# Two state-space heads in one block, one-pass broadcasts, and the decay's differences on VectorE

## Chip, cores and metric

The kernel runs on one core of a Trainium2 chip. The metric is device time in microseconds of one execution. All arithmetic is fp32, or fp32 split into a rounded high part and a low part (the type fp32r) for the large projections.

## What is computed

Two blocks of two layers work on 512 positions of width 1024. The change lies in the first layer of the second block, a state-space mixer with 32 heads of dimension 64 in 4 groups of 8, a state of 128, and the 512 positions in 4 chunks of 128:

```python
dt = softplus(dt + dt_bias);  da = dt * -exp(a_log)
xdt = xs * dt
a_cs = cumsum(da, axis=2)                 # inside each chunk of 128
decay = exp(where(l >= s, a_cs[l] - a_cs[s], -inf))
cb = einsum('bclgn,bcsgn->bcgls', cm, bm)
y_diag = einsum('bcgls,bcgrls,bcsgrp->bclgrp', cb, decay, xdt)
states = einsum('bclgn,bclgr,bclgrp->bcgrpn', bm, exp(a_cs[-1] - a_cs), xdt)
# prev: states carried from chunk to chunk
y_off = einsum('bclgn,bcgrpn,bclgr->bclgrp', cm, prev, exp(a_cs))
y = (y_diag + y_off + d_skip * xs) * silu(z)
y = rms_norm(y, by group of 512 channels) * norm_w;  out = y @ w_out
```

## The kernel before

Five engines work from their own queues, with semaphores between them, and the order on each queue is written out by hand. Channels stand in the 128 partitions and positions in the 512 columns. Weights come through a ring of four blocks; GpSimd splits each into `w_hi` and `w_lo` (L411, L413). A projection tile of 128 channels is 8 steps (`tile_steps`, L840), and a step is three matmuls of 128x512 (L476, L479, L482). The projections z (gate), B, C and x of the mixer are computed one group ahead: `steps_of(ahead, n)` lets n steps run between other work, so that TensorE has something to do while the other engines prepare a head. In group 3 only its own 32 z steps are left.

For each group g, TensorE (L932) transposes B, makes `cb` = B^T C chunk by chunk, broadcasts head 0's cumulated decay, transposes x (`xt`, read by VectorE as `xdt` and `wx`), and makes the three state products (`st`, L957). The sum of the previous group's squares (`norm_sum`) lies between the first and the second of these, because the small products take turns in two PSUM banks, ps6 and ps7: `misc` (L856) lets a product wait until the one before the last has been read from the bank. This stretch, up to the first head, is called the lead below. Then come the 8 heads:

- `spread` (L862, L866 and L867): a column of `ident_r`, repeated 128 times, times `cs_hi` and then times `cs_lo` puts the cumulated decay of one head into all partitions of ps3.
- `decays` on ScalarE (L1432): for each of the 4 chunks a Relu of csT - ps3 into `seg` (L1438), then Exp of ps3 into `ctu` (L1440), which frees ps3, and Exp of -seg (L1442).
- `decayed` on VectorE (L2229): `seg` times `cb`, `ctu` times C.
- `head` on TensorE (L869): for each chunk `xdt` times `seg`, and from the second chunk on the carried state `hst` times `ctu`, added on top; 7 matmuls. An fp32 matmul stands as two records in the trace, so a head has 14. Head r writes partitions 0 to 63 of its bank if r is even and 64 to 127 if it is odd: 64 of the 128 columns of the array.
- `pair` on VectorE (L2207): once two heads are there, adds the skip term, multiplies by Silu of z; ScalarE squares (`gated_square`), VectorE adds up (`add_squares`), and in the next group `norm_root` (L1450) and `group_norm` (L2235, with a reciprocal and four scalings) finish the norm.

`seg` and `ctu` have two buffers. On VectorE the conv taps of the next group (`conv_sides`, L2156) stand in between. ScalarE changes its function table between Exp, Silu and Sqrt; Relu, Copy, Identity and Square need no change.

## Time and profile before

| | us |
|---|---|
| median of 3 runs | 2882.8 (2881.3 to 2891.0) |
| the profiled execution | 2888.4 |
| its span | 2886.6 |
| PE (TensorE matmul) busy | 2800.2, 97% |
| DVE (VectorE) busy | 1727.6, 60% |
| ACT (ScalarE) busy | 791.0, 27% |
| POOL (GpSimd) busy | 1732.4, 60% |

The mixer's four groups lie at 1310 to 1601 us of the span. A busy PE says that matmuls are in flight, not how fast they are issued; matmuls overlap, so their cost on the queue is the distance from one start to the next, not the duration shown. In the chain that ended last TensorE has 84% and VectorE 8%. PEclk is TensorE's granted clock as a share of full speed.

### The profile page before, as it was taken

To read this page: it belongs to the slowest core of one execution; us is meant where nothing else is said; L and a number is where in the kernel's file an instruction comes from. 1 tells how busy PE (TensorE), PEld (TensorE's weight loads), DVE (VectorE), ACT (ScalarE), POOL (GpSimd) and SP (SyncE) were. 2 spreads that over 40 slices of the span, in tenths; PEclk is the share of its full clock that TensorE was granted. 3 is DMA by queue.
4 is the path that set the end of the run, shared out by engine and by line. 5 is a ranking of instruction groups with operands and counts; after the bars stand their busy time and mean duration, and the time that the engine had idled before them with its cause. 6 is when DMAs were issued, how large, how long until landed. Compare 5 with 4: busy or idle time off the path is not lost.

```text
span 2886.6 us, 37343 instructions
## 1 busy us (share of the span) xinstructions
PE 2800.2 (97%) x13446; PEld 2271.8 (79%) x13446; DVE 1727.6 (60%) x1974; ACT 791.0 (27%) x1299; POOL 1732.4 (60%) x984
## 2 busy tenths in 40 slices
PE   8899999999899999999998999999999998999999
PEld 6778888888787888877776778888877776788887
DVE  6886766427867665264665558054567776832635
ACT  3434222103443222025555322010222222310202
POOL 5784666666966666754443548666464443666664
PEclk9999999999999999999999999999999999999999
DMA  4201323332012223322111223222231211222321
GB/s 148 66 30 66 95 94 99 105 97 95 23 54 90 97 95 101 103 84 71 61 64 51 69 71 114 98 95 95 73 108 59 67 60 57 84 100 95 98 98 59
DMA packets 66484, 237.45 MB, mean 82 GB/s; under 512 B 7264, under 2 KB 7520, under 8 KB 66336
## 3 DMA queue, kind: packets, MB, share of 16 engines
q1 hardware_dynamic: 65504, 234.00, 24.8%
q8 instruction: 89, 1.46, 0.2%
q10 hardware_dynamic: 832, 1.51, 0.2%
q14 instruction: 59, 0.48, 0.1%
HBM read 233.38 MB, written 2.10 MB: 82 GB/s over the span
## 4 chain that ended last, share of the span: by engine, by line
PE 84%; DVE 8%; DVEq 3%; issue 3%; ACT 1%; POOL 0%; DMA 0%; ACTq 0%; SPq 0%; POOLq 0%
PE ps L476 25%; PE ps L482 24%; PE ps L479 24%; PE ps L1137 1%; DVE qw L2487 1%; PE ps L879 1%; PE ps L639 1%; DVE ps L1786 1%; PE ps L997 1%; PE ps L989 1%; PE ps L992 1%; PE ps L1173 1%; PE ps L882 1%; PE ps L957 0%; DVEq L1905 0%
## 5 line engine op out<-in xcount | busy, mean ns | idle before, releaser
L411 POOL TENSOR_SCALAR w_hi<-w_raw 128x1024 fp32r<-128x1024 f32 x437 | 482.1, 1103 | 1100.0 <-PE ps L476 1013.0
L413 POOL TENSOR_TENSOR w_lo<-w_raw,w_hi 128x1024 fp32r<-128x1024 f32 x437 | 1100.6, 2519 | 36.5
L476 PE MATMUL ps<-x_hi,w_hi 128*128 128x512 f32 x1864 | 746.2, 400 | 26.3 <-DVE x_lo L1658 5.3
L482 PE MATMUL ps<-x_hi,w_lo 128*128 128x512 f32 x1864 | 730.0, 392 | 0.0
L479 PE MATMUL ps<-x_lo,w_hi 128*128 128x512 f32 x1864 | 729.6, 391 | 0.0
L476 PEld LDWEIGHTS ps<-x_hi,w_hi 128*128 128x128 f32 x1864 | 352.4, 189 | 115.0 <-issue 14.0
L482 PEld LDWEIGHTS ps<-x_hi,w_lo 128*128 128x128 f32 x1864 | 352.2, 189 | 75.6
L479 PEld LDWEIGHTS ps<-x_lo,w_hi 128*128 128x128 f32 x1864 | 352.7, 189 | 74.4 <-issue 4.1
L476 PE MATMUL ps<-a_hi,w_hi 128*128 128x512 f32 x512 | 200.0, 391 | 0.0
L482 PE MATMUL ps<-a_hi,w_lo 128*128 128x512 f32 x512 | 199.2, 389 | 0.0
L479 PE MATMUL ps<-a_lo,w_hi 128*128 128x512 f32 x512 | 199.2, 389 | 0.0
L2311 DVE SCALAR_TENSOR_TENSOR xres<-xres,ps 128x512 f32<-128x512 f32 x32 | 22.0, 688 | 241.1 <-PE ps L482 241.1
L2394 DVE TENSOR_TENSOR sqf<-rl 128x512 f32<-128x512 f32 x64 | 110.0, 1719 | 77.4 <-ACT rl L1561 77.4
L2043 DVE SCALAR_TENSOR_TENSOR yz<-ps,prm,yz 128x511 f32<-128x511 f32 x88 | 65.4, 749 | 150.8 <-ACT yz L1359 150.8
L1561 ACT ACTIVATE rl<-ps 128x512 f32<-128x512 f32 x64 | 38.3, 599 | 402.0 <-PE ps L482 369.8
L2397 DVE TENSOR_TENSOR a_lo<-sqf,a_hi 128x512 f32 x64 | 137.5, 2148 | 14.1 <-issue 13.6
L476 PE MATMUL ps<-f_hi,w_hi 128*128 128x512 f32 x352 | 136.9, 389 | 0.0
L479 PE MATMUL ps<-f_lo,w_hi 128*128 128x512 f32 x352 | 136.9, 389 | 0.0
L482 PE MATMUL ps<-f_hi,w_lo 128*128 128x512 f32 x352 | 136.9, 389 | 0.0
L1786 DVE SCALAR_TENSOR_TENSOR ps<-upad,prm,ps 128x512 f32<-128x512 f32 x168 | 117.4, 749 | 7.1 <-issue 6.9
L2080 DVE TENSOR_TENSOR yz<-sgz,yz 128x512 f32<-128x512 f32 x44 | 113.8, 2586 | 0.0
L476 PE MATMUL ps<-xg_hi,w_hi 128*128 128x512 f32 x256 | 111.6, 436 | 1.6 <-DVE xg_lo L2412 1.6
(424 smaller groups left out, 4678.6 us busy)
## 6 DMA issues: line engine op xcount, KB each, us to landing
w_raw<-wts SPq DMA_DIRECT2D x437, 512.0 KB, 3.4
xres<-xT SPq DMA_DIRECT2D x2, 1024.0 KB, 8.3
outT<-xres SPq DMA_DIRECT2D x8, 256.0 KB, 2.1
pf<-pT ACTq DMA_DIRECT2D x2, 512.0 KB, 3.8
prm<-prm SPq DMA_DIRECT2D x1, 452.0 KB, 3.9
lev<-levels ACTq DMA_DIRECT2D x1, 384.0 KB, 3.9
wtmp<-pos SPq DMA_DIRECT2D x1, 128.0 KB, 3.2
ident<-identity SPq DMA_DIRECT2D x1, 64.0 KB, 10.1
```

Source lines behind the costliest of these rows:

```text
L411: nc.gpsimd.tensor_scalar(w_hi[:, s, :], w_raw[:, s, :], 1.0, 0.0, ALU.mult, ALU.add).then_inc(w_rounded[s], 1)
L413: nc.gpsimd.tensor_tensor(w_lo[:, s, :], w_raw[:, s, :], w_hi[:, s, :].bitcast(F32), ALU.subtract).then_inc(w_split[s], 1)
L476: mm = nc.tensor.matmul(out, whi, xhi, start=first, stop=False)
L479: mm = nc.tensor.matmul(out, whi, xlo, start=False, stop=False)
L482: return nc.tensor.matmul(out, wlo, xhi, start=False, stop=last)
L639: mm = nc.tensor.matmul(ps[5][:, qt * VW:(qt + 1) * VW], p_t[:, h % 2, kt, qt * P:(qt + 1) * P], v_sb[:, kt, h, :], start=kt == 0, stop=kt ...
L1561: AC.activation(rl[:, j % 2, :], ps[j][:, :], ACT.Relu).then_inc(relu_ready, 1)
L1786: ins = V.scalar_tensor_tensor(a if k < CONV_K - 1 else yconv[:, c, :], upad[:, c, k:k + S], w, a, ALU.mult, ALU.add)
L2043: V.scalar_tensor_tensor(yv[:, 1:S], ps[b + z][:, 0:S - 1], prm[:, pc + (L_FW + f * 3), :], yv[:, 1:S], ALU.mult, ALU.add).then_inc(side, 1)
L2080: V.tensor_tensor(yz[i % 2][1], sgz[:, :], yz[i % 2][1], ALU.mult).then_inc(f_ready, 1)
L2394: V.tensor_tensor(sqf[:, j % 2, :], rl[:, j % 2, :], rl[:, j % 2, :], ALU.mult).then_inc(acc_free[j], 1)
L2397: V.tensor_tensor(a_lo[:, q * 4 + j, :], sqf[:, j % 2, :], a_hi[:, q * 4 + j, :].bitcast(F32), ALU.subtract).then_inc(a_split, 1)
```

## The change

The two passes of a broadcast become one: `cs_hl` holds the high part in rows 0 to 31 and the low part in rows 32 to 63, and the columns of `ident_r` have ones in both. VectorE makes all of a head's differences in one instruction (`gap`), ScalarE rectifies them in one Relu over 128x512. The matmuls of two heads stand in one block and alternate between the two halves of the array's columns. `seg` and `ctu` get four buffers, so a broadcast goes out up to two heads before its use. `group_norm` is cut into four parts. To make room for the buffers, some small tiles move into tiles that are free at that time.

```diff
-        seg, _ = at("seg", [P, 2, S])
-        ctu, _ = at("ctu", [P, 2, S - P])
-        cs, _ = at("cs", [P, S])
-        cs_hi, _ = at("cs_hi", [P, S], F32R)
-        cs_lo, _ = at("cs_lo", [P, S], F32R)
+        seg, _ = at("seg", [P, 4, S])
+        ctu, _ = at("ctu", [P, 4, S - P])
+        cs_hl, _ = at("cs_hl", [P, S], F32R)
...
             def spread(g, r):
                 k = GH * g + r
                 pe.wait_ge(csb_read, k)
+                pe.wait_ge(gap_ready, k)
                 col = ident_r[:, k:k + 1].to_broadcast([P, P])
-                nc.tensor.matmul(ps[3][:, :], col, cs_hi[:, :], start=True, stop=False)
-                nc.tensor.matmul(ps[3][:, :], col, cs_lo[:, :], start=False, stop=True).then_inc(csb_done, 1)
+                nc.tensor.matmul(ps[3][:, :], col, cs_hl[:, :], start=True, stop=True).then_inc(csb_done, 1)
...
+            def head_pair(g, p):
+                n, out = GT * g + p, ps[4 + p % 2]
+                pe.wait_ge(m_ready, 2 * n + 2)
...
+                both = [(r, slice((r % 2) * HD, (r % 2 + 1) * HD)) for r in (2 * p, 2 * p + 1)]
                 for tt in range(TT):
+                    c = slice(tt * P, (tt + 1) * P)
+                    for r, rows in both:
+                        mm = nc.tensor.matmul(out[rows, c], xdt[:, tt, r * HD:(r + 1) * HD], seg[:, r % 4, c],
+                                              start=True, stop=tt == 0)
                     if tt:
+                        for r, rows in both:
+                            mm = nc.tensor.matmul(out[rows, c], hst[:, tt - 1, r * HD:(r + 1) * HD],
+                                                  ctu[:, r % 4, (tt - 1) * P:tt * P], start=False, stop=True)
                 mm.then_inc(yh_done, 1)
...
+                    if c == 0:
+                        spread(g, 1)
                     if c == 0 and g:
                         norm_sum(g - 1)
...
-                for r in range(GH):
-                    steps_of(ahead, (4 if g else 3) if some else 2)
-                    if r + 1 < GH:
-                        spread(g, r + 1)
-                    steps_of(ahead, (4 if g else 3) if some else 1)
-                    head(g, r)
-            steps_of(ahead, len(TILES) * KD)
+                for p in range(GT):
+                    share = [4 if g else 3] * 4 if some else [2, 1, 2, 1]
+                    steps_of(ahead, share[0])
+                    if p + 1 < GT:
+                        spread(g, 2 * p + 2)
+                    steps_of(ahead, share[1])
+                    if some or p + 1 < GT:
+                        head_pair(g, p)
+                    steps_of(ahead, share[2])
+                    if p + 1 < GT:
+                        spread(g, 2 * p + 3)
+                    steps_of(ahead, share[3])
+            head_pair(GROUPS - 1, GT - 1)
...
             def decays(g, r):
...
-                if k >= 2:
-                    act.wait_ge(yh_done, k - 1)
-                for tt in range(TT):
-                    AC.activation(seg[:, r % 2, tt * P:(tt + 1) * P], ps[3][:, tt * P:(tt + 1) * P], ACT.Relu,
-                                  bias=csT[:, tt, k:k + 1], scale=-1.0)
-                AC.activation(ctu[:, r % 2, :], ps[3][:, P:], ACT.Exp).then_inc(csb_read, 1)
-                act.wait_ge(csb_read, k + 1)
-                AC.activation(seg[:, r % 2, :], seg[:, r % 2, :], ACT.Exp, scale=-1.0).then_inc(dec_ready, 1)
+                if k >= 4:
+                    act.wait_ge(yh_done, k // 2 - 1)
+                AC.activation(ctu[:, r % 4, :], ps[3][:, P:], ACT.Exp).then_inc(csb_read, 1)
+                act.wait_ge(gap_ready, k + 1)
+                AC.activation(seg[:, r % 4, :], seg[:, r % 4, :], ACT.Relu)
+                act.drain()
+                AC.activation(seg[:, r % 4, :], seg[:, r % 4, :], ACT.Exp, scale=-1.0).then_inc(dec_ready, 1)
...
+                decays(g, 1)
                 if g:
                     norm_root(g - 1)
...
-            V.tensor_copy(ident_r[:, :], ident[:, 0:SH])
+            V.tensor_tensor(ident_r[:, :], ident[:, 0:SH], ident[:, SH:2 * SH], ALU.add)
...
-            V.tensor_tensor(cs_lo[:, :], cs[:, :], cs_hi[:, :].bitcast(F32), ALU.subtract).then_inc(small_dve, 1)
+            V.tensor_tensor(cs_hl[SH:2 * SH, :], cs[0:SH, :], cs_hl[0:SH, :].bitcast(F32), ALU.subtract).then_inc(small_dve, 1)
...
+            def gap(g, r):
+                k = GH * g + r
+                dve.wait_ge(csb_read, k + 1)
+                if k >= 4:
+                    dve.wait_ge(yh_done, k // 2 - 1)
+                V.tensor_tensor(seg[:, r % 4, :].rearrange("p (t q) -> p t q", t=TT), csT[:, :, k:k + 1].to_broadcast([P, TT, P]),
+                                ps[3][:, :].rearrange("p (t q) -> p t q", t=TT), ALU.subtract).then_inc(gap_ready, 1)
...
+                gap(g, 0)
                 decayed(g, 0)
+                gap(g, 1)
                 for c in (1, 2):
...
+                decayed(g, 1)
+                gap(g, 2)
                 for r in range(GH):
+                    if r >= 2 and r % 2 == 0:
+                        pair(g, r // 2 - 1)
+                    if 1 <= r < GH - 1:
+                        decayed(g, r + 1)
                     if g + 1 < GROUPS and r >= 3:
                         conv_sides(g + 1, CONV_T[r - 3])
-                    if r >= 2 and r % 2 == 0:
-                        pair(g, r // 2 - 1)
-                    if r + 1 < GH:
-                        decayed(g, r + 1)
                     if r in (5, 7):
                         add_squares(g, (r - 3) // 2)
-                    if r == 1 and g:
-                        group_norm(g - 1)
+                    if 1 <= r < GH - 2:
+                        gap(g, r + 2)
+                    if 1 <= r <= GT and g:
+                        group_norm(g - 1, r - 1)
```

Three places show what moves. TensorE first, the matmuls of heads in group 1, from a projection matmul to the next one (ps4 is the bank of the heads' output; a count says how many alike follow each other). Before, one head:

```order
L482 MATMUL ps0<-x_hi_53,w_lo_51 128x512
L879 MATMUL ps4<-seg_116,xdt_109 64x128 x2
L882 MATMUL ps4<-ctu_117,hst_111 64x128
L879 MATMUL ps4<-seg_116,xdt_109 64x128
L882 MATMUL ps4<-ctu_117,hst_111 64x128
L879 MATMUL ps4<-seg_116,xdt_109 64x128
L882 MATMUL ps4<-ctu_117,hst_111 64x128
L476 MATMUL ps0<-x_hi_53,w_hi_50 128x512
```

After, two heads:

```order
L482 MATMUL ps2<-x_hi_53,w_lo_51 128x512
L881 MATMUL ps4<-seg_116,xdt_109 64x128 x4
L885 MATMUL ps4<-ctu_117,hst_111 64x128 x2
L881 MATMUL ps4<-seg_116,xdt_109 64x128 x2
L885 MATMUL ps4<-ctu_117,hst_111 64x128 x2
L881 MATMUL ps4<-seg_116,xdt_109 64x128 x2
L885 MATMUL ps4<-ctu_117,hst_111 64x128 x2
L476 MATMUL ps2<-x_hi_53,w_hi_50 128x512
```

The same rows now hold two heads: each count is doubled, and within a count the output alternates between partitions 0 to 63 and 64 to 127.

ScalarE in the lead of group 1, from head 0's decay to the root of the previous group's norm, with the semaphores that a row waits for. Before:

```order
L1438 ACTIVATE seg<-ps,csT 128x128 [waits yh_done,csb_done]
L1438 ACTIVATE seg<-ps,csT 128x128 x3
L1440 ACT_TABLE_LOAD
L1440 ACTIVATE ctu<-ps 128x384
L1442 ACTIVATE seg<-seg 128x512 [waits csb_read]
L1496 ACTIVATE hst<-ps 128x512 [waits misc_done]
L1453 ACT_TABLE_LOAD
L1453 ACTIVATE root<-ps,consts 128x512 [waits misc_done]
```

After:

```order
L1448 ACT_TABLE_LOAD [waits yh_done]
L1448 ACTIVATE ctu<-ps 128x384 [waits csb_done]
L1450 ACTIVATE seg<-seg 128x512 [waits gap_ready]
L1452 ACTIVATE seg<-seg 128x512
L1506 ACTIVATE hst<-ps 128x512 [waits misc_done]
L1448 ACTIVATE ctu<-ps 128x384 [waits yh_done,csb_done]
L1450 ACTIVATE seg<-seg 128x512 [waits gap_ready]
L1452 ACTIVATE seg<-seg 128x512
L1463 ACT_TABLE_LOAD
L1463 ACTIVATE root<-ps,consts 128x512 [waits misc_done]
```

Head 1's three rows now stand ahead of the table load and the root, and head 0's Relu waits for VectorE (`gap_ready`).

VectorE in group 1, from the last state addition to the second pair of heads' products. Before:

```order
L2278 TENSOR_TENSOR hst<-hst,ps 128x512 [waits misc_done]
L2232 TENSOR_TENSOR seg<-seg,cb 128x512 [waits dec_ready]
L2233 TENSOR_TENSOR ctu<-ctu,cT 128x384
L2232 TENSOR_TENSOR seg<-seg,cb 128x512 [waits dec_ready]
L2233 TENSOR_TENSOR ctu<-ctu,cT 128x384
L2237 RECIPROCAL rstd<-root 128x512 [waits root2_ready]
L2241 SCALAR_TENSOR_TENSOR y<-y,prm,rstd 128x512 x4
L2211 SCALAR_TENSOR_TENSOR xs<-xs,prm,ps 128x512 [waits sz_ready,yh_done]
L2214 TENSOR_TENSOR y<-xs,y 128x512
L2232 TENSOR_TENSOR seg<-seg,cb 128x512 [waits dec_ready]
L2233 TENSOR_TENSOR ctu<-ctu,cT 128x384
```

After:

```order
L2299 TENSOR_TENSOR hst<-hst,ps 128x512 [waits misc_done]
L2251 TENSOR_TENSOR seg<-seg,cb 128x512 [waits dec_ready]
L2252 TENSOR_TENSOR ctu<-ctu,cT 128x384
L2245 TENSOR_TENSOR seg<-csT,ps 128x512 [waits yh_done,csb_read]
L2251 TENSOR_TENSOR seg<-seg,cb 128x512 [waits dec_ready]
L2252 TENSOR_TENSOR ctu<-ctu,cT 128x384
L2245 TENSOR_TENSOR seg<-csT,ps 128x512 [waits yh_done,csb_read]
L2257 RECIPROCAL rstd<-root 128x512 [waits root2_ready]
L2260 SCALAR_TENSOR_TENSOR y<-y,prm,rstd 128x512
L2222 SCALAR_TENSOR_TENSOR xs<-xs,prm,ps 128x512 [waits sz_ready,yh_done]
L2225 TENSOR_TENSOR y<-xs,y 128x512
L2251 TENSOR_TENSOR seg<-seg,cb 128x512 [waits dec_ready]
```

The subtractions (seg<-csT,ps) are new; the reciprocal and the first scaling stand behind head 3's subtraction and ahead of the first pair's output, and the other three scalings are spread over the following heads.

## Rows read from the trace of the kernel before

**Rows 1.** Windows: length; busy PE, PEld, DVE, ACT, POOL; PEclk; DMA
```profile
1310.13:1378.76 68.63, 68.51 (x355) 54.10 (x353) 39.07 (x51) 38.63 (x76) 27.51 (x16) 1.00 0.21 69
1378.76:1460.16 81.40, 80.56 (x405) 63.57 (x404) 50.79 (x64) 43.99 (x81) 36.20 (x20) 1.00 0.20 64
...
1541.59:1601.48 59.89, 52.34 (x260) 39.00 (x259) 34.21 (x46) 36.71 (x70) 14.17 (x8) 0.91 0.11 38
```

**Rows 2.** PE in time, one head of group 1: start us, us, instruction
```profile
1427.25 0.39 PE L482 MATMUL ps<-x_hi,w_lo 128*128 128x512 f32 x1
1427.57 0.65 PE L879 MATMUL ps<-seg,xdt 128*64 128x128 f32 x4
...
1429.24 0.50 PE L476 MATMUL ps<-x_hi,w_hi 128*128 128x512 f32 x1
1429.58 0.39 PE L479 MATMUL ps<-x_lo,w_hi 128*128 128x512 f32 x1
```

**Rows 3.** PE in time, next broadcast and matmul behind
```profile
1432.11 0.40 PE L866 MATMUL ps<-cs_hi,ident_r 128*128 128x512 f32 x1
...
1432.58 0.39 PE L476 MATMUL ps<-x_hi,w_hi 128*128 128x512 f32 x1
```

**Rows 4.** PE in time, later mixer: alternating halves, then one half
```profile
2199.64 0.69 PE L1137 MATMUL ps<-qw,kw 128*64 128x64 f32 x16
2200.25 0.50 PE L476 MATMUL ps<-xg_hi,w_hi 128*128 128x512 f32 x1
...
2202.65 0.68 PE L1150 MATMUL ps<-qw,kw 128*64 128x64 f32 x8
2203.26 0.50 PE L476 MATMUL ps<-xg_hi,w_hi 128*128 128x512 f32 x1
```

**Rows 5.** Lines: shapes, count; busy us, mean ns; idle before, releaser
```profile
L1438 ACT ACTIVATE seg<-ps,csT 128x128 f32<-128x128 f32 x128 | 36.6, 368 | 68.3 <-PE ps L867 68.0 <-issue 0.2
...
L1442 ACT ACTIVATE seg<-seg 128x512 f32<-128x512 f32 x32 | 20.2, 632 | 1.0
...
L1440 ACT ACTIVATE ctu<-ps 128x384 f32<-128x384 f32 x32 | 16.0, 501 | 0.2
...
L2232 DVE TENSOR_TENSOR seg<-seg,cb 128x512 f32<-128x512 f32 x32 | 25.0, 781 | 77.3 <-ACT seg L1442 76.8
...
L2233 DVE TENSOR_TENSOR ctu<-ctu,cT 128x384 f32<-128x384 f32 x32 | 19.3, 604 | 0.0
```

**Rows 6.** Single lines: count; ns at least/median/at most; first and last start; form
```profile
L2264 DVE TENSOR_TENSOR xdt<-ps,dtT x16: 691/692/693, 1317.9 to 1554.5; 128x512 f32<-128x512 f32 x16
...
L2214 DVE TENSOR_TENSOR y<-xs,y x16: 691/693/2782, 1341.4 to 1603.8; 128x512 f32<-128x512 f32 x16
```

**Rows 7.** ACT in order of time, lead of group 1
```profile
1392.85 0.60 ACT L1496 ACTIVATE hst<-ps 128x512 f32<-128x512 f32 x1 [3.55 <-PE ps L957]
1393.55 1.28 ACT L1453 ACT_TABLE_LOAD   x1
1394.84 0.69 ACT L1453 ACTIVATE root<-ps,consts 128x512 f32<-128x512 f32 x1
```

**Rows 8.** DVE in order of time, lead of group 1
```profile
1391.70 0.69 DVE L2264 TENSOR_TENSOR xdt<-ps,dtT 128x512 f32<-128x512 f32 x1
```

**Rows 9.** PE in time, group 1: first transpose, third state product, head
```profile
1378.76 0.55 PE L937 MATMUL ps<-ident,bT 128*128 128x128 f32 x3
...
1396.46 1.02 PE L957 MATMUL ps<-wx,b_l 128*128 128x512 f32 x2
...
1404.04 0.65 PE L879 MATMUL ps<-seg,xdt 128*64 128x128 f32 x4
```

**Rows 10.** PE in time, group 3: fourth head and matmul behind
```profile
1580.26 1.12 PE L879 MATMUL ps<-seg,xdt 128*64 128x128 f32 x4 [3.92 <-DVE ctu L2233]
...
1583.26 0.50 PE L476 MATMUL ps<-x_hi,w_hi 128*128 128x512 f32 x1
```

**Rows 11.** DVE in order of time, group 3: the reciprocal
```profile
1570.14 3.35 DVE L2237 RECIPROCAL rstd<-root 128x512 f32<-128x512 f32 x1
```

55 lines of the change are left out of this document (25 added, 30 removed).

## The prediction, made before the kernel ran

> **What bounds the kernel now.** I read the stretch table first. The change only touches the state-space mixer, which fills 291 us of the span in four groups [rows 1]. In groups 0 and 1 TensorE is busy for 68.5 of 68.6 and 80.6 of 81.4 us (group 2 repeats group 1), while VectorE is at 39 and 51 us and ScalarE at 39 and 44 us: there TensorE is the bound, and what is taken off its queue shortens the group, as long as nobody makes it wait. Group 3 is another case: 52.3 of 59.9 us at a granted clock of 0.91. It has no next group's projections to fill with, so TensorE already waits there for the decay factors.
>
> Then the price of the parts on TensorE. Every head has a block of 14 matmul records between projection matmuls. The last projection matmul before it starts at 1427.25, the first behind it at 1429.24 and the next at 1429.58 [rows 2]; less two ordinary pitches of 0.23, the block costs 1429.58 - 1427.25 - 0.46 = 1.87 us. Every head also has a broadcast of two passes, 1432.11 to 1432.58, so 0.23 each [rows 3]. A projection step, three matmuls at that pitch, is 0.69 us.
>
> **Part 1: broadcasts of one pass.** The high and the low part stand in rows 0 to 31 and 32 to 63 of one operand, and the selecting column has two ones. It removes 32 passes of 0.23 us: 7.4 us, all on TensorE's queue.
>
> **Part 2: two heads in one block.** A head's output uses half of the array's columns (128*64); the halves of heads 2p and 2p+1 now alternate. Does the chip run them side by side? The trace of before holds both patterns in the later mixer. Line 1137 alternates between the halves: 16 records start at 2199.64 and the following matmul at 2200.25, 0.61 us. Line 1150 stays in one half: 8 records of the same shape take 2202.65 to 2203.26, also 0.61 us [rows 4]. So twice the records go through in the same time, and I price the block of 28 records like that of 14: 1.87 us. It saves 16 x 1.87 = 29.9 us. The bounds: no overlap leaves only the fixed part of one block per pair, 1.87 - 1.67 = 0.20 us, so 3.2 us in all; the upper end is 29.9. I take the upper one, because rows 4 are the same chip, operand type and record kind; what differs is 128 moving columns for 64, and that a second matmul adds to what the first wrote.
>
> The Trainium skill speaks against this: TensorE: Matmul & The Clock Gate, "Part 3: Packing small matmuls", says that a weight load overlaps with running matmuls only when the row group differs, and column halves share their row group. By that rule the pair would be serial, as in rival C below. Rows 4 say otherwise, since each of line 1137's records has a weight load of its own.
>
> Parts 1 and 2 together are 8 x 0.23 + 4 x 1.87 = 9.3 us for each group, 37.3 in all, if nobody waits.
>
> **Part 3: the decay's differences.** Removed on ScalarE: four Relus of 0.37 us for each head; added: one Relu over 128x512 on SBUF, which I price like the Exp of that form, 0.63 (bounds: 0.60, line 1496's copy out of PSUM, and 0.69, the root) [rows 5, 7]. Added on VectorE: one subtraction for each head with one operand in PSUM. The nearest row is line 2264 (PSUM times a broadcast), 0.69 us at least and at most; the other end is line 2214, two SBUF operands, 0.69 at the median but 2.78 at most [rows 6]. I take 0.69. On load alone this is hidden: 5.5 us on VectorE for each group, which makes some 56 of 72. What counts is the chain. Before, it was broadcast, ScalarE, VectorE, TensorE; now it is broadcast, Exp of the cross term 0.50, subtraction 0.69, Relu 0.63, Exp 0.63, the two products 1.2 (0.78 and 0.60 busy, their pipelines overlapping) [rows 5, 6]: with an estimated 0.4 until the broadcast is seen and 0.1 for each hand-over some 4.4 us. The four buffers for `seg` let a broadcast go out up to eight steps ahead. In groups 1 and 2 a pair gives it 12 steps and two broadcasts, 8.5 us; in group 0 some 6.5 us; both cover 4.4 and the previous pair's output (two instructions with a drain between, twice 0.69 and the hand-overs: 1.6 us) that VectorE puts between. Group 1 and 2's second pair also has the reciprocal, 3.35 us [rows 11], in VectorE's queue between the subtraction of head 3 and its product. That comes to some 11.4 us from the block's end, and TensorE arrives at 11.4 as well: 0.6 us of waiting for each of these groups, an estimate for products that run longer beside GpSimd.
>
> **Part 4: the lead of each group, where the gain is given back.** ScalarE's order now has the whole of head 1's decay between the copy of the first state and the square root of the previous group's norm. That root reads the PSUM bank which the third state product needs, so TensorE stands before that product. Before, in us from the group's first transpose (1378.76): last `xdt` product from 12.9 to 13.6 [rows 8]; root from 16.1 to 16.8 [rows 7]; third state product at 17.7; first head at 25.3 [rows 9]. After: subtraction of head 0 until 14.3, Relu and Exp until 15.6, state copy 0.60 until 16.25, Exp of head 1's cross term until 16.75, its subtraction (behind head 0's two products) 17.5, Relu and Exp 18.9, table load 1.28 and root 0.69 [rows 7] until 20.9, third state product 21.0. From there to the first block it was 25.3 - 17.7 = 7.6, now 7.35 with one broadcast pass less: 28.3. That is 3.0 later, although a net 0.2 of the passes counted in part 1 lies in this stretch: 3.2 us are given back. TensorE, which is through with the second state product and its step at some 17.9, idles 3.1 of them in one piece. After an idle of 3.92 us in group 3 it ran at the lower of its two clocks (1.2 for 2.4 GHz): the block of 14 records took 1580.26 to 1583.26, 3.0 for 1.67 [rows 10]. That would be 1.3 us more; since 3.1 is shorter than 3.92, I book 1.0 (bounds 0 and 1.3). Group 0 has no root in its lead, only the copy of the first state, behind head 0's Exp: 0.3 us, and 0.3 at the broadcast of head 1, which now waits for the subtraction of head 0.
>
> **Group 3.** Lead: the same chain, begun 0.2 earlier by the shorter broadcast, ends in the third state product at 20.8, the first block at 24.1 at full clock, and at 25.5 with the half clock behind nearly 4 us of idling. The pairs: the interval from the end of one block to the next is bounded by the chain: broadcast after two steps (1.4), subtraction done 3.1, previous pair's output 4.6, products 5.85. The second pair has the reciprocal and one scaling (4.0) between: 9.9. The third has one scaling: 6.9. The last is bounded by TensorE's own nine steps and broadcast, 6.4. With four blocks of 1.87 that is 30.8, with the half clock again after the long wait (1.3) and 0.5 for longer products 32.6. Sum 58.1 for 59.9: a gain of 1.8 us.
>
> **The sum.** Group 0: -9.3 + 0.6 and 0.3 for its last pair, whose queue on VectorE is the fullest, = -8.4. Groups 1 and 2: -9.3 + 3.2 + 1.0 + 0.6 = -4.5 each. Group 3: -1.8. In all -19.2 us. What follows (output projection) starts behind the last z tile's Silu as before and moves along; the setup (a sum for a copy of 128x32, a subtraction of 32 rows for 128) has a wait behind it and counts nothing. The profiled execution took 2888.4 us with its span of 2886.6; the median is 2882.8, so I subtract from that: **2864 us**.
>
> **Rivals.**
> A, the forecast: the halves overlap, the leads cost 3 us and some clock. 2858 to 2870. Chance 0.52.
> B, cheaper leads: the clock stays high and products run undisturbed. Groups 0 to 3 then give 9.0, 6.1, 6.1 and 4.6: 25.8, so 2857 and down to 2851. For it: 3.1 us of idling may not be enough to lower the clock. Against: group 3 shows 0.91 already. Chance 0.22.
> C, it doesn't do what it says: no overlap of the halves once a second matmul adds on top. Then 29.9 becomes 3.2, and the sum is +7.5; 1 to 3 us of that are waits that a longer block fills, so 2887. Against: rows 4. Chance 0.12.
> D, slower: the subtraction behaves like line 2214's slow case, held up beside GpSimd's weight splitting, 2.78 for 0.69. Two of them stand in each lead's chain (4.2 us for each of four leads), one in the second pair of groups 1 and 2 (2.1 each) and one in each of three pairs in group 3 (6.3): 16.8 + 4.2 + 6.3 = 27.3, so +8.1: 2891. It decides from 0.69 + 2.09 x 19.2/27.3 = 2.2 us for one subtraction. Against: 16 of 16 instructions with a PSUM operand stay at 0.69 [rows 6]. Chance 0.06.
> The rest, 0.08, is the forecast with hand-overs 0.2 to 0.3 us longer each, 2871 to 2882.
>
> **The numbers.** A, B and the rest are 0.82: the range is 2850 to 2882. A measurement can tell 0.3% (8.6 us) from no change: faster is A, B and half of the rest, 0.78; same is C, a third of D and the other half, 0.18; slower 0.04.
>
> **What would show it.** Right: the blocks at line 881 and 885 have 28 records in about 1.7 us; group 0 takes about 60 us, groups 1 and 2 about 77, group 3 about 58; line 1450 and 1452 near 0.63 each, line 2245 at 0.69; an idle piece of 3 us on TensorE before the third state product of groups 1 to 3, released by the root. Wrong: blocks of 3.2 us (C), line 2245 above 2 us (D), or a TensorE wait at every block of groups 0 to 2, which would mean that the chain of 4.4 us is really over 6.

## The result, and the profile after

The changed kernel took 2891.3 us (median of 10 runs) beside 2885.9 for the kernel before in the same session: a ratio of 1.0019, 95% interval 1.001 to 1.0028. So it is slightly slower, by less than 0.3%, where 2864 was forecast and 2882 was the upper end of the range. The profiled execution has a span of 2888.9 us. (One of the ten runs, a disturbed one of 3931 us, is left out of the ratio; the median of the other nine is 2890.7.)

The page of the kernel after: busy time of each engine, and the chain that ended last. VectorE rose from 8% to 12% of the chain, its queue from 3% to 5%.

```profile
PE 2768.9 (96%) x13414; PEld 2246.2 (78%) x13414; DVE 1769.6 (61%) x2006; ACT 772.6 (27%) x1201; POOL 1733.0 (60%) x984
...
PE 78%; DVE 12%; DVEq 5%; issue 3%; ACT 2%; POOL 0%; ACTq 0%; DMA 0%; SPq 0%; POOLq 0%
```

TensorE is busy for 31 us less, most of the 37 us that the forecast took off its queue with parts 1 and 2, and yet the end came no earlier: the time turned into waiting. Windows of the kernel after for groups 0, 1 and 3 (columns as in [rows 1]; group 2 repeats group 1):

```profile
1310.30:1379.19 68.89, 61.33 (x346) 48.11 (x345) 49.64 (x59) 34.36 (x50) 29.01 (x16) 0.98 0.21 68
1379.19:1461.57 82.38, 73.36 (x396) 57.37 (x395) 61.81 (x70) 39.42 (x56) 36.33 (x20) 0.98 0.19 59
...
1544.00:1606.60 62.60, 44.76 (x253) 32.65 (x251) 44.65 (x57) 32.67 (x49) 14.36 (x8) 0.86 0.14 43
```

The groups took 68.6, 81.4, 81.4 and 59.9 us before and 68.9, 82.4, 82.4 and 62.6 now: +5.0 us, where -19.2 was forecast. In these windows TensorE was idle for 9.4 us (length less busy time, [rows 1] with group 2) and is idle for 43.4. Behind the mixer TensorE waits 0.8 us less than before. The rest is what differs from run to run: outside the mixer's groups the profiled executions differ by a few us, whatever the change, so this document compares groups where it can.

One block of two heads, PE in time (start, us, instruction):

```profile
1422.30 0.66 PE L881 MATMUL ps<-seg,xdt 128*64 128x128 f32 x8 [1.35 <-DVE ctu L2252]
1422.79 0.39 PE L885 MATMUL ps<-ctu,hst 128*64 128x128 f32 x4
...
1423.98 0.50 PE L476 MATMUL ps<-x_hi,w_hi 128*128 128x512 f32 x1
```

The eight and four records of the first two rows are followed by four more rows of four. That is 28 records in 1423.98 - 1422.30 = 1.68 us, where by the same measure 14 records took as long before (1427.57 to 1429.24, 1.67) [rows 2]. The halves overlap in full. But the first row also has what was not foreseen: 1.35 us of waiting for VectorE's product, and the like stands before every block of groups 1 and 2.

Windows from block to block in group 1, first of the kernel before (two heads each), then of the kernel after:

```profile
1404.04:1419.72 15.68, 15.68 (x82) 12.62 (x81) 9.34 (x9) 8.18 (x17) 6.93 (x4) 1.00 0.22 73
1419.72:1435.42 15.70, 15.70 (x81) 12.60 (x80) 12.64 (x16) 7.78 (x18) 7.26 (x4) 1.00 0.21 65
1435.42:1451.13 15.71, 15.71 (x81) 12.61 (x81) 8.86 (x14) 10.11 (x20) 7.20 (x4) 1.00 0.21 63
```

```profile
1407.58:1422.30 14.72, 13.37 (x80) 10.83 (x79) 10.13 (x9) 5.31 (x8) 6.90 (x4) 1.00 0.31 105
1422.30:1437.05 14.75, 13.39 (x78) 10.74 (x79) 12.18 (x14) 6.70 (x11) 7.46 (x4) 1.00 0.24 73
1437.05:1452.71 15.66, 13.13 (x78) 10.63 (x78) 14.11 (x17) 8.65 (x13) 7.21 (x4) 1.00 0.21 67
```

TensorE's own need fell from 15.7 to 13.3 us (second column), as forecast; the interval didn't follow. In the third, VectorE is busy for 14.1 us, which is more than TensorE needs. In the first it is busy for only 10.1 and TensorE waits all the same. The broadcasts of heads 2 and 3, which the block at 1422.30 uses, and VectorE in time show why:

```profile
1404.52 0.40 PE L867 MATMUL ps<-cs_hl,ident_r 128*128 128x512 f32 x1
1412.13 0.40 PE L867 MATMUL ps<-cs_hl,ident_r 128*128 128x512 f32 x1
...
1407.58 0.69 DVE L2251 TENSOR_TENSOR seg<-seg,cb 128x512 f32<-128x512 f32 x1 [1.41 <-ACT seg L1452]
1408.19 0.55 DVE L2252 TENSOR_TENSOR ctu<-ctu,cT 128x384 f32<-128x384 f32 x1
1413.09 0.69 DVE L2245 TENSOR_TENSOR seg<-csT,ps 128x512 f32<-128x512 f32 x1 [4.35 <-ACT ctu L1448]
1413.70 3.34 DVE L2257 RECIPROCAL rstd<-root 128x512 f32<-128x512 f32 x1
1417.12 2.60 DVE L2260 SCALAR_TENSOR_TENSOR y<-y,prm,rstd 128x512 f32<-128x512 f32 x1
1419.65 0.73 DVE L2222 SCALAR_TENSOR_TENSOR xs<-xs,prm,ps 128x512 f32<-128x512 f32 x1
1420.48 0.69 DVE L2225 TENSOR_TENSOR y<-xs,y 128x512 f32<-128x512 f32 x1
1421.09 0.68 DVE L2251 TENSOR_TENSOR seg<-seg,cb 128x512 f32<-128x512 f32 x1
1421.69 0.55 DVE L2252 TENSOR_TENSOR ctu<-ctu,cT 128x384 f32<-128x384 f32 x1
```

The queue is in order. Its head is the subtraction of head 3 (L2245). It waits until ScalarE has read the broadcast (L1448), and the broadcast comes only at 1412.13, so VectorE stands 4.35 us with the reciprocal behind it. Then the reciprocal, a scaling and the previous pair's output all run between that subtraction and the product of the same head. From its broadcast (1412.13) to the block (1422.30) the odd head takes 10.2 us.

The new and the old operations from 1310 to 1600 us, by line (busy us, mean ns, idle before; the last head's products fall behind 1600):

```profile
L2252 DVE TENSOR_TENSOR ctu<-ctu,cT 128x384 f32<-128x384 f32 x31 | 29.7, 959 | 0.0
L2251 DVE TENSOR_TENSOR seg<-seg,cb 128x512 f32<-128x512 f32 x31 | 28.9, 933 | 18.8 <-ACT seg L1452 18.2
L2245 DVE TENSOR_TENSOR seg<-csT,ps 128x512 f32<-128x512 f32 x32 | 22.0, 687 | 22.8 <-ACT ctu L1448 20.0 <-issue 2.7
...
L1450 ACT ACTIVATE seg<-seg 128x512 f32<-128x512 f32 x32 | 20.2, 632 | 73.8 <-DVE seg L2245 73.8
```

Each price is as forecast (0.687 and 0.632). But VectorE stands 20 us at subtractions, for ScalarE's reading of the broadcast, and 18 at products, and the two products, which nobody touched, have grown from 781 and 604 ns [rows 5] to 933 and 959: of all 64, 12 take more than 1 us, where 5 did before.

### The profile page after: what moved, and what is told of

It is laid out like the page before. It is cut to its first block, busy times and chain, and to the rows that moved or that the text cites. A ratio compares the mean times of both kernels' runs of the same rounds, so it can differ in the third digit from the quotient of the medians.

```text
span 2888.9 us, 37303 instructions
## 1 busy us (share of the span) xinstructions
PE 2768.9 (96%) x13414; PEld 2246.2 (78%) x13414; DVE 1769.6 (61%) x2006; ACT 772.6 (27%) x1201; POOL 1733.0 (60%) x984
## 4 chain that ended last, share of the span: by engine, by line
PE 78%; DVE 12%; DVEq 5%; issue 3%; ACT 2%; POOL 0%; ACTq 0%; DMA 0%; SPq 0%; POOLq 0%
PE ps L476 23%; PE ps L482 23%; PE ps L479 23%; PE ps L1148 1%; DVE qw L2513 1%; DVE ps L1797 1%; PE ps L639 1%; DVEq L2224 1%; PE ps L1008 1%; PE ps L1184 1%; PE ps L1000 1%; PE ps L1003 1%; DVE seg L2251 1%; DVE ctu L2252 1%; DVE seg L2245 0%
## 5 line engine op out<-in xcount | busy, mean ns | idle before, releaser
L2054 DVE SCALAR_TENSOR_TENSOR yz<-ps,prm,yz 128x511 f32<-128x511 f32 x88 | 65.4, 749 | 151.0 <-ACT yz L1370 151.0
L2423 DVE TENSOR_TENSOR a_lo<-sqf,a_hi 128x512 f32 x64 | 137.4, 2147 | 14.1 <-issue 13.6
## 6 DMA issues: line engine op xcount, KB each, us to landing
ident<-identity SPq DMA_DIRECT2D x1, 64.0 KB, 10.2
```

The costliest lines, as they stand in the source:

```text
L2054: V.scalar_tensor_tensor(yv[:, 1:S], ps[b + z][:, 0:S - 1], prm[:, pc + (L_FW + f * 3), :], yv[:, 1:S], ALU.mult, ALU.add).then_inc(side, 1)
L2423: V.tensor_tensor(a_lo[:, q * 4 + j, :], sqf[:, j % 2, :], a_hi[:, q * 4 + j, :].bitcast(F32), ALU.subtract).then_inc(a_split, 1)
```

## The experiments

Eighteen kernels, in five sessions; the kernel before ran in each (2885.8, 2885.2, 2886.3, 2886.2 and 2888.1 us). Ratios are to it, with their 95% interval. The expectations weigh several theories. "Q" means at first that the subtraction's place in VectorE's queue decides, and from e9 on that this queue is full, wherever the work stands. The code shown is cut to what matters ("..." marks a cut).

**e1: the four Relus back on ScalarE, no subtraction.** One-pass broadcasts and blocks of two heads stay.

```diff
-                pe.wait_ge(gap_ready, k)
...
+                for tt in range(TT):
+                    AC.activation(seg[:, r % 4, tt * P:(tt + 1) * P], ps[3][:, tt * P:(tt + 1) * P], ACT.Relu,
+                                  bias=csT[:, tt, k:k + 1], scale=-1.0)
                 AC.activation(ctu[:, r % 4, :], ps[3][:, P:], ACT.Exp).then_inc(csb_read, 1)
-                act.wait_ge(gap_ready, k + 1)
-                AC.activation(seg[:, r % 4, :], seg[:, r % 4, :], ACT.Relu)
-                act.drain()
+                act.wait_ge(csb_read, k + 1)
...
-                gap(g, 0)
...
```

> The changed kernel with its part 3 undone: no subtraction on VectorE, ScalarE again makes four Relus of 128x128 out of PSUM for each head, then both Exps; pairs of heads, one-pass broadcasts, four buffers and all positions stay. Theory Q (the subtraction stands in VectorE's queue behind products and convolution taps, so a broadcast waits there and the chain passes that queue twice): the waits of TensorE before the blocks (28.6 us in the changed kernel) fall under 8 us, groups 0 to 2 take about 59.5, 74 and 74 us where the changed kernel takes 68.9, 82.4 and 82.5, and the time falls to 2857 to 2865. Rival L (the lead with the root behind head 1's decay is what eats the gain, with the lowered clock after it): at most 5 us better than the changed kernel, 2886 or more. Rival S (VectorE is simply full; one instruction of 0.69 less for each head): 32 x 0.69 = 22 us off its queue, of which only the waiting part counts, 2875 to 2882.

Measured: 2866.6 us, ratio 0.9934 [0.991, 0.9958]. Just above its range, but 25 us below after. The first interval of group 1, and VectorE at its start:

```profile
1404.28:1417.57 13.29, 13.29 (x79) 10.81 (x78) 11.43 (x9) 8.82 (x18) 7.37 (x4) 1.00 0.23 80
```

```profile
1405.89 0.55 DVE L2252 TENSOR_TENSOR ctu<-ctu,cT 128x384 f32<-128x384 f32 x1
1406.36 3.35 DVE L2257 RECIPROCAL rstd<-root 128x512 f32<-128x512 f32 x1
```

The reciprocal starts at once, and TensorE waits for nothing, although VectorE is busier here (11.43 us) than in the same interval of after (10.13). So the sum of VectorE's work doesn't explain the first interval.

**e2: the root first.** The kernel after, with ScalarE's root ahead of head 1's decays and, on VectorE, head 1's subtraction behind the state additions.

```diff
+                if g:
+                    norm_root(g - 1)
                 decays(g, 1)
                 if g:
-                    norm_root(g - 1)
                     z_silu(g, 0)
...
-                gap(g, 1)
                 for c in (1, 2):
...
+                gap(g, 1)
                 decayed(g, 1)
```

> The changed kernel with only the lead put back in order: on ScalarE the root of the previous group's norm stands ahead of head 1's decay, on VectorE head 1's subtraction behind the state additions. Theory Q: the idle piece of 2.9 us before the third state product goes in groups 1 to 3, but the loop behind it stays as slow as it was, so 6 to 9 us at most, 2882 to 2886. Rival L: it gives back most of what was expected, 2872 or less.

Measured: 2885.0 us, 1.0001 [0.999, 1.0013]: 6 us below after. The third state product waits 0.27 for 2.92 us, and the waits before the blocks are the same (1.37, 1.31, 2.53). By group: groups 1 and 2 take 78.1 us each, 4.3 less than after, but group 0, which has no root to bring forward, takes 71.6, 2.7 more: the later subtraction of head 1 costs there.

**e3: both.**

> Both edits: Relus on ScalarE and the root ahead of head 1's decay. If Q and the lead are separate and add up, it has nearly all of the 37 us that parts 1 and 2 take off TensorE's queue in groups 0 to 2 (28 us) and 4 to 7 us in group 3: 2850 to 2856, below both kernels. If the root was hidden anyway once the decay is quick, it equals the run with the Relus alone.

Measured: 2865.9 us, 0.9923 [0.9899, 0.9948]: a miss. Groups 1 and 2 fell to 71.9 us (from 73.4 in e1), with no wait at a block, but groups 0 and 3 hardly moved against e1 (66.6 and 60.4 there, 65.4 and 60.6 here), where the chain through ScalarE and VectorE still decides (a wait of 5.0 us in group 3 and 3.3 in group 0).

**e4: one-pass broadcasts alone, on the kernel before.**

```diff
-                nc.tensor.matmul(ps[3][:, :], col, cs_hi[:, :], start=True, stop=False)
-                nc.tensor.matmul(ps[3][:, :], col, cs_lo[:, :], start=False, stop=True).then_inc(csb_done, 1)
+                nc.tensor.matmul(ps[3][:, :], col, cs_hl[:, :], start=True, stop=True).then_inc(csb_done, 1)
```

> The kernel before with the one-pass broadcast alone. 32 passes of 0.23 us are off TensorE's queue: 7.4 us less where TensorE is the bound (groups 0 to 2, 5.5 us), some of the rest in group 3. 2877 to 2881 if the pass is priced rightly; no change (2884 to 2888) if the broadcasts were hidden in waiting.

Measured: 2877.2 us, 0.9971 [0.9959, 0.9983]: 8.6 us for the forecast's 7.4. The groups themselves are 1.8, 1.9, 2.0 and 0.9 us shorter, 6.7 in all.

**e5 and e6: GpSimd's low parts taken away**, from after and from before. The low parts of the mixer's weights are then left out of the products; this asks what GpSimd's presence costs VectorE.

```diff
+                e = 8 if NB1 + B_G + 4 <= n < NB1 + B_SO else BLK
-                nc.gpsimd.tensor_tensor(w_lo[:, s, :], w_raw[:, s, :], w_hi[:, s, :].bitcast(F32),
+                nc.gpsimd.tensor_tensor(w_lo[:, s, 0:e], w_raw[:, s, 0:e], w_hi[:, s, 0:e].bitcast(F32),
```

> The changed kernel with GpSimd's second instruction cut to 8 of 1024 columns for the weight blocks of the mixer's input projections: the low parts of these weights are left out, so TensorE multiplies with stale ones; the number of matmuls, steps and waits is the same. Theory G (VectorE's products with two SBUF operands are held up beside GpSimd, mean 0.93 and 0.95 us for 0.69 and 0.55 alone, and the new queue cannot absorb it): those means fall to 0.69 and 0.55, groups 0 to 2 lose their waits in the loop and take about 62, 77 and 77 us, and the time falls by 14 to 22 us to 2869 to 2877. Theory Q alone (position in VectorE's queue): the means fall all the same, but the groups shorten by at most 2 us each, 2884 or more.

> The same cut in the kernel before, as the base for the other run (the low parts of the same weights left out). Before, the factors are asked for late and TensorE is the bound, so both theories expect no change beyond 3 us, 2882 to 2887; a fall of 8 us or more would mean that the cut helps by itself, through the transfers or through TensorE's wait for weights.

Measured: 2864.2 us, 0.9934 [0.9918, 0.9951], and 2879.9, 0.9987 [0.9978, 0.9997]. After loses 27 us and before 5, both more than was expected. Some 4 us of each lie ahead of the mixer's groups, where TensorE waits once for a PSUM bank that VectorE's convolution taps read. Before, and then e6:

```profile
1284.66 0.80 PE L476 MATMUL ps<-x_hi,w_hi 128*128 128x512 f32 x1 [4.45 <-DVEq L2161]
```

```profile
1283.27 0.50 PE L477 MATMUL ps<-x_hi,w_hi 128*128 128x512 f32 x1 [0.32 <-DVEq L2162]
```

This wait is 4.49 us in after and 0.32 in e5. In the four groups together the hold-ups cost the kernel before 1.0 us (all of it in group 3) and the kernel after 21: groups 0 to 2 take 61.1, 75.3 and 75.3 us in e5 for 68.9, 82.4 and 82.4, and group 3 takes 63.8 for 62.6, so nothing is won there. In e5, every interval of groups 1 and 2 is TensorE's 13.3 (13.0 for the last). By line, e5:

```profile
L2252 DVE TENSOR_TENSOR seg<-seg,cb 128x512 f32<-128x512 f32 x32 | 24.7, 772 | 18.9 <-ACT seg L1453 18.4
L2253 DVE TENSOR_TENSOR ctu<-ctu,cT 128x384 f32<-128x384 f32 x32 | 23.2, 724 | 0.0
L2246 DVE TENSOR_TENSOR seg<-csT,ps 128x512 f32<-128x512 f32 x32 | 22.0, 687 | 25.7 <-ACT ctu L1449 23.3 <-issue 2.2
```

The products, with two operands in SBUF, fell to 772 and 724 ns (not to the 0.69 and 0.55 us that were expected; outside of the mixer's input projections the weight blocks are still split in full); the subtraction, with one in PSUM, stays at 687 in both. VectorE stands at the subtractions no shorter than in after (23.3 us for 20.0). So in groups 1 and 2 the standing alone doesn't hold TensorE, and in the kernel before the hold-up alone doesn't: it takes both. In group 3 it doesn't take the hold-ups: the waits before its blocks are the same in e5 (0.95, 6.28, 1.92, 3.21 us) as in after (0.82, 6.28, 1.77, 3.22).

**e7: the subtraction ahead of the conv taps**, all else as in after.

```diff
                     if 1 <= r < GH - 1:
                         decayed(g, r + 1)
+                    if 1 <= r < GH - 2:
+                        gap(g, r + 2)
                     if g + 1 < GROUPS and r >= 3:
                         conv_sides(g + 1, CONV_T[r - 3])
```

> The changed kernel with one position changed on VectorE: the subtraction for head r+2 stands right behind the products of head r+1, ahead of the convolution taps (2.4 us each) and of the sums of squares. Theory Q: the broadcasts no longer wait for taps, the waits before the third and fourth block go in groups 0 to 2; 5 to 10 us better than the changed kernel, 2881 to 2886. Rival: VectorE now stands still for the broadcast instead of doing taps, and the taps come late; no change or slower, 2890 to 2895.

Measured: 2891.1 us, 1.0019 [1.0008, 1.003]. My theory missed and the rival held. The subtraction of head 5 now ends early, but the taps (2.38 us) then lie between it and the product: they moved from one side of it to the other, and both sides are inside the odd head's way.

**e8: e3, and the products at the head of the loop.** The lines shown are the difference from e3.

```diff
+                    if 1 <= r < GH - 1:
+                        decayed(g, r + 1)
                     if r >= 2 and r % 2 == 0:
                         pair(g, r // 2 - 1)
-                    if 1 <= r < GH - 1:
-                        decayed(g, r + 1)
+                    if r in (6, 7):
+                        add_squares(g, r - 5)
                     if g + 1 < GROUPS and r >= 3:
                         conv_sides(g + 1, CONV_T[r - 3])
-                    if r in (5, 7):
-                        add_squares(g, (r - 3) // 2)
-                    if 1 <= r <= GT and g:
-                        group_norm(g - 1, r - 1)
+                    if 2 <= r <= GT + 1 and g:
+                        group_norm(g - 1, r - 2)
```

> The run with Relus on ScalarE and the root first, with VectorE's loop reordered: a head's products stand ahead of the previous pair's output, and the reciprocal with the four scalings moves behind head 3's products. Its waits before blocks were 1.0 and 3.3 us in group 0 and 0.6, 2.0, 5.0, 0.7 and 2.1 us in group 3. Both theories: group 0 from 65.4 to about 61, groups 1 and 2 stay at 72, group 3 from 60.6 to 53 to 56; 2854 to 2862. If another wait takes their place (ScalarE's Silus, the accumulator banks), 2864 or more.

Measured: 2864.6 us, 0.9931 [0.9915, 0.9948]. Group 3 came down from 60.6 to 55.7 us and group 0 from 65.4 to 64.4. The medians of e3 and e8 differ by 1 us, but they come from different sessions and e3's five runs spread from 2854.8 to 2867.2; the two profiled executions differ by 4.2 us (2866.8 and 2862.6).

**e9 and e10: half of the subtractions**, the even heads' or the odd heads'. The others' Relus are ScalarE's, as in e1. In e10 the condition is `r % 2 == 1`.

```diff
+        def by_vector(g, r):
+            return r % 2 == 0
```

> After, with the difference by VectorE for the even heads only; the odd heads' four Relu are ScalarE's, out of PSUM. Theory Q (VectorE's queue): between two blocks of groups 1 and 2 VectorE is 11.8 us busy of 13.0 and 14.1 of 15.7, the queue is full, and each subtraction out of it counts the same whichever head it belongs to. Half of them gone gives half of what all gave (2891.3 to 2866.6): 2876 to 2882, and e10 the same within 3 us. Rival H (the hand-over): a block waits for its odd head alone, whose broadcast comes 10 us before it and the even head's some 4 us earlier; only the odd head's trip through two engines counts. Then this kernel gives nearly all of it, 2866 to 2872, and e10 next to nothing.

> The mirror of the run before: difference by VectorE for the odd heads, the four Relu by ScalarE for the even ones. Theory Q: 2876 to 2882, within 3 us of the run before. Rival H: 2886 to 2892.

Measured: 2871.5 us, 0.994 [0.9921, 0.9958], and 2887.0, 0.9998 [0.9986, 1.001]. The same amount of work, 16 subtractions, costs some 5 us with the even heads (against e1, and not clear of noise: the intervals of e1 and e9 overlap) and 20 with the odd. The full-queue theory is out for these two; the hand-over theory holds with both numbers. By group the odd heads cost in groups 1 and 2 (79.2 and 80.9 us for 76.3 and 74.9 in e9) and 3 (63.5 for 61.7); in group 0 it is the other way round (66.1 in e10, 68.4 in e9, 66.6 in e1). Intervals of group 1, e9 and then e10:

```profile
1409.43:1422.72 13.29, 13.29 (x79) 10.81 (x78) 10.48 (x10) 7.18 (x13) 7.37 (x4) 1.00 0.24 78
1422.72:1436.02 13.30, 13.30 (x80) 10.83 (x79) 11.83 (x16) 6.01 (x13) 7.38 (x4) 1.00 0.25 80
1436.02:1449.06 13.04, 13.04 (x78) 10.63 (x77) 11.21 (x12) 8.83 (x15) 7.21 (x4) 1.00 0.24 78
```

```profile
1406.12:1420.84 14.72, 13.37 (x80) 10.82 (x79) 10.19 (x10) 6.29 (x12) 6.90 (x4) 1.00 0.32 105
1420.84:1435.58 14.74, 13.37 (x79) 10.82 (x79) 11.84 (x13) 7.17 (x15) 7.22 (x4) 1.00 0.23 72
1435.58:1451.21 15.63, 13.10 (x77) 10.63 (x78) 14.76 (x16) 8.97 (x16) 7.22 (x4) 1.00 0.20 67
```

With 10.48 and 10.19, 11.83 and 11.84 us of VectorE's work the first runs at TensorE's pace and the second waits as in after. The odd head is the one that counts because its broadcast goes out behind the previous block, 7.6 us after the even one's (1404.52 and 1412.13 in after), and both are used by the same block.

**e11: e1 and e5 together** (the low parts left out again).

> Both unloadings of VectorE together: the four Relu per head by ScalarE, and GpSimd's low parts of the mixer's weights cut to 8 of 1024 columns (those low parts are left out of the products, so part of the computation is missing). Each alone gave 25 and 27 us. If both act on one bound, VectorE's full queue, TensorE takes over once it is open, and together they give little more than one: 2857 to 2864. Rival: two separate costs, which add up: 2839 to 2846.

Measured: 2851.4 us, 0.988 [0.9856, 0.9904]. Each alone gave 25 and 27, both 40: neither theory's number. In groups 1 and 2 they overlap fully (TensorE's 13.3 with either), in groups 0 and 3 they don't: group 0 is 59.4 us, against 68.9 in after, 66.6 in e1 and 61.1 in e5, close to the sum of both gains, and group 3 is 55.6, against 62.6, 60.4 and 63.8, more than the sum. In e11 TensorE is idle for 0.1 us in group 0. Some 4 us of the 40 lie ahead of the groups, as in e5.

**e12: e8, with the even heads of group 3 by VectorE.**

> The kernel of e8 (four Relu by ScalarE, root first, products at the head of the loop), and in the last group the even heads' difference by VectorE as in after. In e8 TensorE stood 6.5 us in the last group for ScalarE's chain and 6.2 for VectorE's products. Splitting the work between the two: 2858 to 2864 if ScalarE's four passes were what the last group waits for; 2865 or more if VectorE's queue is as full there.

Measured: 2864.4 us, 0.9921 [0.9896, 0.9947], the same as e8 and between the two ranges. TensorE's longest wait for ScalarE in group 3 is 3.8 us for 3.1, so taking half of the four passes off ScalarE doesn't shorten it.

**e13: a clear way for the odd head.** The kernel after, all subtractions by VectorE; its other work stands where it falls inside even heads.

```diff
+                    if g + 1 < GROUPS and r in (3, 5):
+                        conv_sides(g + 1, CONV_T[r - 3])
+                    if 1 <= r < GH - 1:
+                        decayed(g, r + 1)
                     if r >= 2 and r % 2 == 0:
                         pair(g, r // 2 - 1)
-                    if 1 <= r < GH - 1:
-                        decayed(g, r + 1)
-                    if g + 1 < GROUPS and r >= 3:
+                    if g + 1 < GROUPS and r in (4, 6, 7):
                         conv_sides(g + 1, CONV_T[r - 3])
...
                     if 1 <= r < GH - 2:
                         gap(g, r + 2)
-                    if 1 <= r <= GT and g:
+                    if r in (2, 4) and g:
+                        group_norm(g - 1, r - 2)
                         group_norm(g - 1, r - 1)
+                    if r in (6, 7):
+                        add_squares(g, r - 5)
```

> After, every subtraction still by VectorE, but its other work in the loop is written into the gaps of the even heads: nothing stands between the odd head's subtraction and its products. e9 and e10 showed that the odd head's trip decides. Theory J (what lengthens the trip is the taps, norms and squares queued inside it): the waits ahead of blocks in groups 1 and 2, 5.2 us each, and part of those in group 0 go: 2878 to 2884. Theory Q (the queue is full, so the work only moves, and VectorE now stands 1.4 us per pair for Relu and Exp): 2889 to 2896.

Measured: 2895.5 us, 1.0032 [1.0013, 1.0052], in the range that was given to the full queue. The intervals, and the wait in the second:

```profile
1408.25:1421.54 13.29, 13.29 (x79) 10.81 (x79) 6.56 (x7) 5.07 (x8) 7.18 (x4) 1.00 0.22 73
1421.54:1438.02 16.48, 13.53 (x79) 10.74 (x79) 13.03 (x13) 5.94 (x9) 6.89 (x4) 1.00 0.26 92
...
1434.88 0.47 PE L867 MATMUL ps<-cs_hl,ident_r 128*128 128x512 f32 x1 [2.95 <-DVE seg L2245]
```

The first interval is free, as theory J (the odd head's trip) says. In the second, the work put ahead of head 5's subtraction makes that late, and now the next broadcast waits for it: there is one PSUM bank (ps3) for all broadcasts, and since the change it comes free only with VectorE's subtraction.

**e14 and e15: this order with the root first**, the even heads' subtractions by VectorE (e14), or none (e15).

> The loop order of the run before, the root ahead of head 1's decays, and the odd heads' Relu by ScalarE, the even heads' difference by VectorE. The odd head passes VectorE's queue once, and the even one has time. Theory J: no wait at blocks of groups 1 and 2, lead without its 2.5: 2860 to 2866. Theory Q: 2867 to 2874.

> The same loop order and root, all Relu by ScalarE, no subtraction on VectorE. Theory J and theory Q both: as e8, 2861 to 2867; lower than 2861 only if the squares and taps behind the products also held group 3.

Measured: 2870.7 us, 0.9951 [0.9937, 0.9965], above the range of theory J and in the one of the full queue; and 2866.2, 0.9934 [0.9913, 0.9955], within. Without subtractions the order as such costs little: 2866.2 us for 2864.6 in e8, though group 3 takes 58.6 us for 55.7.

**e16 to e18: the reciprocal put where VectorE stood**, ahead of head 3's subtraction, and the scalings spread; e17 with the root first, e18 also with the odd Relus by ScalarE. The lines shown are the difference of e16 from e13.

```diff
+                    if r == 1 and g:
+                        group_norm(g - 1, 0)
                     if 1 <= r < GH - 2:
                         gap(g, r + 2)
-                    if r in (2, 4) and g:
-                        group_norm(g - 1, r - 2)
-                        group_norm(g - 1, r - 1)
+                    if r in (2, 4, 6) and g:
+                        group_norm(g - 1, r // 2)
```

> The order of e13, all subtractions by VectorE, but the reciprocal and the first scaling of the group before stand ahead of head 3's subtraction, where VectorE stands 4.36 us for that head's broadcast, and the other three scalings are spread over heads 2, 4 and 6. Theory S (the in-order queue stands at a subtraction whose broadcast has not come, and the work behind it then falls between an odd head's subtraction and its product, or in e13 ahead of the next even subtraction): the first two intervals of groups 1 and 2 are TensorE's own 13.3, the third at most 14.5; 2876 to 2883. Theory Q (the queue is full wherever the work stands): 2889 or more.

> The run before with the root ahead of head 1's decays, which took 2.65 of the 2.92 us out of each lead in e2 (and gave 6 us). Theory S: the two add, 2869 to 2877. If blocks only wait longer instead: 2876 to 2883.

> The same, the odd heads' Relu by ScalarE. Theory S: nothing waits in groups 1 and 2: 2862 to 2867, as e8 and e12. Above 2869: the even subtractions still cost there.

Measured: 2904.2 us, 1.0052 [1.0035, 1.0068]; 2901.1, 1.0046 [1.0029, 1.0063]; 2878.6, 0.9968 [0.9955, 0.998]. All three missed what theory S gave them; e16 is in the open range (2889 or more) of the full queue. Intervals of e16:

```profile
1407.77:1421.06 13.29, 13.29 (x79) 10.82 (x78) 11.71 (x9) 4.24 (x6) 7.23 (x4) 1.00 0.21 75
1421.06:1437.23 16.17, 13.54 (x80) 10.74 (x79) 11.92 (x12) 6.65 (x10) 7.17 (x4) 1.00 0.29 95
1437.23:1452.76 15.53, 13.12 (x78) 10.63 (x77) 13.47 (x15) 9.08 (x13) 7.21 (x4) 1.00 0.20 68
```

The first is free with the reciprocal in it. The second is no better than in e13 although 3.3 us of work left it: VectorE is 11.92 us busy and stands for the other 4.2, 2.50 at an even subtraction for its broadcast and 1.40 for ScalarE's Relu and Exp of the odd head, with two hold-ups beside GpSimd (2.83 and 2.71 us for 0.75 and 0.55) in what is left. Group 3 also grew, to 68.6 us from 60.5 in e13. One part of that stands in its trace, at the first transposes of x in group 3:

```profile
1554.43 0.66 PE L953 MATMUL ps<-ident,xs 128*128 128x128 f32 x4 [2.23 <-ACT xs L1436]
```

In group 2 the last scaling (2.97 us) and a sum of squares (2.39) are held up ahead of the last convolution taps, which start at 1551.3, so the channels of x come late. In e18 groups 2 and 3 both begin with such a wait (2.24 and 2.22 us). The rest of the growth was not followed up.

None of the orders that I tried frees all three intervals with both heads' subtractions on VectorE, and whether there is one stays open. All of them move work on VectorE and ScalarE. The other way to shorten the odd head's way, a broadcast that TensorE sends out ahead of the block and not behind it, was not tried.

## Why the prediction was wrong

**The parts on TensorE were right.** Part 1: 8.6 us measured alone (e4) for 7.4. Part 2: 1.68 us for 28 records, and where TensorE doesn't wait, as in e1, a block costs 1.88 us on the queue by the forecast's measure (1.87), so the 29.9 us are real. TensorE's need per interval fell from 15.7 to 13.3, which is 9.6 per group with four pairs (forecast 9.3). Where nothing waits the saving arrives: groups 1 and 2 are 9.5 us shorter than before in e3, and group 0 is 9.2 shorter in e11. Rival C is out, and with it, for this shape, the rule of the Trainium skill that was weighed there (TensorE: Matmul & The Clock Gate, "Part 3: Packing small matmuls"): by it these loads should have been serial, and they are not. The same section of the Trainium skill also has three column tiles in its table of measured speedups, at 2.38 times, so it doesn't say that column tiles run one after the other; the prediction weighed the one sentence alone.

**Part 4, the lead, was right in size.** ScalarE and PE in time in group 1 of the kernel after:

```profile
1399.34 0.69 ACT L1463 ACTIVATE root<-ps,consts 128x512 f32<-128x512 f32 x1
...
1400.12 1.13 PE L960 MATMUL ps<-wx,b_l 128*128 128x512 f32 x2 [2.92 <-ACTq L1464]
```

From the group's first transpose at 1379.19 the third state product is at 20.9 (forecast 21.0) and the first block at 28.4 (28.3). The idle piece is 2.92 us (3.1). The 1.0 us that I booked for half clock directly behind it didn't come: the granted clock from 1400.12 to the block is 1.00. It came later in the group, behind the last wait before a block, where the clock was 0.60. e2 shows that this belongs to the lead's price too: without the lead's wait, the same wait of 2.53 us leaves the clock up.

```profile
1457.32:1461.61 4.29, 4.29 (x39) 3.68 (x40) 3.85 (x6) 3.04 (x4) 1.87 (x2) 1.00 0.01 4
```

So e2 gives the lead a price of 4.3 us in each of groups 1 and 2, for the forecast's 4.2 (3.2 and 1.0). That the two agree so well is in part luck, since the clock fell in another place. The whole of e2 is 6 us faster than after, because group 0 lost 2.7.

**Part 3 failed: the change of engine was priced by VectorE's average load and by a chain that left out most of VectorE's queue.** Two sentences fail. The first: "On load alone this is hidden: 5.5 us on VectorE for each group, which makes some 56 of 72." The group took 61.8 us of VectorE, and the average over it says nothing on the intervals, which hold 10.1, 12.2 and 14.1 of TensorE's 13.3. The 11 us over the 50.8 of before are the subtractions (5.5) and what was held up longer beside GpSimd: products (3.7), sums of squares (3.8) and scalings (1.9), with 2.5 less at the pairs' outputs.

The second: the chain of 4.4 us that a budget of 8.5 covers (12 steps and two broadcasts add up to 8.7), with only the previous pair's output put between, and in the second pair the reciprocal. In VectorE's queue there also stand the conv taps (2.38 us for each head from the fourth on), a scaling (0.75 to 2.6; the prediction counted it in group 3 alone) and a subtraction that itself waits for its broadcast. The way of the odd head is 10.2 us, which is the "really over 6" that the prediction named as its refutation, and the waits came where it said: before nine of the twelve blocks of groups 0 to 2.

**By group.** "Booked" is what the forecast allowed for. Group 1: forecast -4.5, measured +1.0. The waits before blocks are 1.35, 1.36 and 2.53 us, 5.2 in all for the 0.6 booked, which is 4.6 of the miss of 5.5; the clock is most of the rest. Behind the last of these waits the granted clock fell. The window behind the lead's wait, and then the one behind the last wait before a block:

```profile
1400.12:1407.58 7.46, 7.46 (x30) 5.55 (x30) 3.38 (x4) 5.53 (x7) 3.95 (x2) 1.00 0.04 7
...
1452.71:1457.00 4.29, 4.29 (x32) 3.63 (x33) 3.85 (x6) 3.04 (x4) 0.78 (x1) 0.60 0.02 4
```

0.60 over 4.29 us is 3.4 us at the lower level (1.2 GHz), so 1.7 us lost where 1.0 was booked. Group 2 repeats this. Group 0: -8.4 forecast, +0.3 measured; it waits 0.92, 0.96 and 4.17 us before blocks and 1.39 for a bank, 7.4 in all, and its last block runs at half clock. Group 3: -1.8 forecast, +2.7 measured; the intervals between its blocks are 12.8, 9.8 and 11.6 us for 11.8, 8.8 and 8.3 forecast (and 1.8 booked beside them), and its first block comes 26.7 us into the group for 25.5. The last interval was said to be bounded by TensorE's own nine steps; TensorE waits 3.22 us in it for VectorE's product. The longest waits of groups 0 and 3, PE in time:

```profile
1371.80 1.12 PE L881 MATMUL ps<-seg,xdt 128*64 128x128 f32 x8 [4.17 <-DVE ctu L2252]
...
1583.49 1.12 PE L881 MATMUL ps<-seg,xdt 128*64 128x128 f32 x8 [6.28 <-DVE ctu L2252]
```

The misses, 8.7, 5.5, 5.5 and 4.5, make 24.2 of the 24.6 us between the forecast change (-19.2) and the measured one (+5.4).

**Rival D named the right neighbour and the wrong instruction.** It had 2891 us, and 2891.3 was measured, but by a mechanism that didn't occur: the subtraction stayed at 0.687. What GpSimd holds up are the instructions with two operands in SBUF, which were there before and had slack then. The change took the slack: TensorE arrives 2.4 us earlier per pair, and the subtraction makes their turn come later. e5 and e6 price this: in the mixer's groups the hold-ups cost 1 us in the kernel before and 21 in the kernel after, and some 4 us ahead of the groups in both. That rival D's number was met is luck. The Trainium skill describes such a lock between the two engines (SBUF — State Buffer, "SBUF: two separate sides"): the engine that comes second waits out the other's whole instruction, and VectorE is touched only with two SBUF inputs or in a two-port mode. These traces agree: 0.55 us for a product alone and 2.75 for one that starts at 1426.39 in after, beside a GpSimd instruction of 2.72 that started at 1426.01, and no change with a PSUM operand. That VectorE's instructions in a two-port mode are touched is shown by no run here.

**What is shown and what isn't.** Shown: undoing part 3 gives back 25 us (e1), and in groups 1 to 3 the odd heads' subtractions cost more than the even heads' (e9, e10). Shown: removing the hold-ups gives 22 us in groups 0 to 2 and nothing in group 3 (e5, which leaves out part of the computation), and neither alone closes groups 0 and 3 (e11). Shown for the orders that I tried: other work ahead of the odd subtraction delays the next broadcast, other work behind it the block (e7, e13, e16). The full queue was refuted by e9 and e10 but met the numbers of e13, e14 and e16, so how much of VectorE's time could be given to subtractions in a better order is open. Not shown: which step of VectorE or ScalarE sets group 3, where e1, e5 and e10 each leave most of the waits, why the even heads cost more in group 0, and most of what lengthened group 3 in e16.

The best complete versions are those whose Relus are made by ScalarE out of PSUM (in e12 all but those of group 3's even heads): e1, e3, e8, e12 and e15 take 2864.4 to 2866.6 us, 0.7 to 0.8% below the kernel before, and the runs don't rank them. The forecast's 2864 us was thus within the reach of parts 1 and 2, but not with its own part 3.

## What to carry to other kernels

When a step is handed to an engine that works in order, don't price it by that engine's average load. Write out what stands in its queue between the step's input and its output, add the longest holds that the trace shows for each of those instructions, and count the standing of the new instruction itself, since all that is queued behind it moves with it. And look which of the items is on the way that ends last: here 16 subtractions cost some 5 us on one set of heads and 20 on the other.

## What the runs showed of the hardware that was not expected

- The clock doesn't go by the length of the last idle piece alone. Behind a wait of 2.92 us the granted clock stayed at 1.00 for the next 7.46 us (after, 1400.12), and behind one of 2.53 us it was 0.60 over 4.29 us (1452.71). In e2, which has the same wait of 2.53 us and the same 1.37 and 1.31 before it, but 0.27 for the 2.92 in the lead, it stayed at 1.00 (1457.32). In e13 it fell behind the lead's 2.92 us (0.81 over the next 9.12).
- Two fp32 matmul streams in the two column halves, each adding a second matmul onto the first, overlap in full: from the first of 28 records to the matmul behind them it is 1.68 us, where 14 took 1.67.
- A VectorE product of 0.55 us was held to 2.75 beside a GpSimd instruction of 2.72, while a subtraction with one operand in PSUM and the same shape of output kept 0.687 us as a mean of 32.
